# Moving four gate projections of a joint attention layer behind queries and keys on one Trainium2 core

## The reference, cut to what matters

```python
def heads_ab(pp, cq_gain, ckv_gain, w_uq, w_ukv, q_gain, k_gain, qg_gain, kg_gain):
    cq, ckv, kr, gq, gk, gv, gate = split_cols(pp, AB_SPLIT)
    qa = (rmsnorm(cq, cq_gain) @ w_uq).reshape(lead + (MLA_HEADS, MLA_NOPE + MLA_ROPE))
    kv = (rmsnorm(ckv, ckv_gain) @ w_ukv).reshape(lead + (MLA_HEADS, MLA_NOPE + MLA_V))
    ...
    return rmsnorm(qa, q_gain), rmsnorm(ka, k_gain), va, qb, kb, vb, gate

    qa, ka, va, qb, kb, vb, g = heads_ab(h @ w_in, *wts)
    qac, kac, vac, qbc, kbc, vbc, gc = heads_ab(hc @ w_in, *wts)
    ...
    oa = joint_dense_attention(qa, ka, va, kac, vac).reshape(b, s, -1)
    ob = joint_dense_attention(qb, kb, vb, kbc, vbc).reshape(b, s, -1)
    mix = jnp.concatenate([oa, ob], axis=-1) * jax.nn.silu(g)
    x = x + gate * (mix @ w_out)
```

## Time and profile before

| what | value |
|---|---|
| time, median of 3 runs | 1003.01 us (1002.25 to 1006.51) |
| span of the profiled execution | 1002.4 us |
| TensorE busy in the span | 942.2 us (94%) |
| share of the chain that ended last: PE, DVE, ACT, DMA | 84%, 5%, 4%, 4% |
| PE from 664.93 to 727.16 us (gates `ga4`, `ga5` to `ga7`) | busy throughout |
| PE from 727.16 to 736.27 us (transposes of queries and keys) | 5.06 us busy of 9.11 |
| granted clock of TensorE from 736.27 to 760 us, mean | 0.86 |

### The profile page before, as it was taken

The page is one execution under the profiler, slowest core; times in us unless marked ns, Lnnn a source line. Parts: engine busy times, 40 slices in busy tenths (PEclk is TensorE's granted clock), DMA queues, the critical chain, the costliest instruction groups (busy, mean ns, idle before and its releaser), DMA issues.

```text
span 1002.4 us, 11949 instructions
## 1 busy us (share of the span) xinstructions
PE 942.2 (94%) x4380; PEld 513.4 (51%) x4381; DVE 373.4 (37%) x838; ACT 308.4 (31%) x700; POOL 31.7 (3%) x54
## 2 busy tenths in 40 slices
PE   3899989999999899997999999999989999999998
PEld 1455446546454335442355446455766456577763
DVE  1200497634271110522122321610855633236452
ACT  3211533332131121342233321311466632125420
POOL 0100200000000000000000002000000000000000
PEclk9999999999999999999999999999989999999999
DMA  9966482489696699899799999414226734423501
GB/s 349 364 212 229 50 314 99 157 297 336 215 365 229 216 334 393 297 396 396 276 398 383 398 396 295 178 48 157 85 84 239 215 93 168 161 91 101 133 19 42
DMA packets 105693, 230.75 MB, mean 230 GB/s; under 512 B 3124, under 2 KB 6504, under 8 KB 105496
## 3 DMA queue, kind: packets, MB, share of 16 engines
q1 hardware_dynamic: 100288, 217.85, 61.5%
q0 software_dynamic: 2208, 7.37, 2.6%
q10 hardware_dynamic: 3128, 4.62, 1.4%
HBM read 224.31 MB, written 5.51 MB: 229 GB/s over the span
## 4 chain that ended last, share of the span: by engine, by line
PE 84%; DVE 5%; ACT 4%; DMA 4%; issue 2%; SPq 1%; ACTq 0%; DVEq 0%
PE bank L633 24%; PE bank L900 12%; PE bank L647 9%; PE bank L913 6%; PE bank L930 4%; PE bank L599 3%; PE bank L1208 3%; DMA arena<-in_w_mod_dram 3%; PE bank L1137 3%; PE bank L1227 2%; PE bank L1218 2%; PE bank L829 1%; PE bank L925 1%; PE bank L762 1%; PE bank L983 1%
## 5 line engine op out<-in xcount | busy, mean ns | idle before, releaser
L633 PE MATMUL bank<-arena 128*128 128x512 f32 (+3 forms) x592 | 236.6, 558 | 1.9 <-DVE arena L2687 1.0
L633 PEld LDWEIGHTS bank<-arena 128*128 128x128 f32 x592 | 111.2, 190 | 117.9 <-issue 109.1
L900 PE MATMUL bank<-arena 128*64 128x512 f32 x512 | 113.0, 593 | 3.4 <-issue 3.4
L647 PE MATMUL bank<-arena 128*128 128x256 f32 (+1 forms) x384 | 99.3, 417 | 2.8 <-ACT arena L1935 1.5
L647 PEld LDWEIGHTS bank<-arena 128*128 128x128 f32 x384 | 72.1, 190 | 30.9 <-issue 21.7
L900 PEld LDWEIGHTS bank<-arena 128*64 128x64 f32 x512 | 38.8, 137 | 73.9 <-issue 73.3
L913 PE MATMUL bank<-arena,con 128*64 128x512 f32 x272 | 65.0, 621 | 4.6 <-ACT con L1838 4.0
L599 PE MATMUL bank<-arena,silu_c 128*32 128x512 f32 x384 | 48.8, 630 | 9.5 <-DMA arena<-in_w_mod_dram 6.7
L1739 ACT ACTIVATE con<-bank 128x256 f32<-128x256 f32 x17 | 6.5, 383 | 137.3 <-PE bank L900 137.3
L2358 DVE TENSOR_TENSOR con<-con,bank 128x256 f32<-128x256 f32 x17 | 7.2, 421 | 109.5 <-ACT con L1743 109.5
L913 PEld LDWEIGHTS bank<-arena,con 128*64 128x64 f32 x272 | 21.4, 143 | 37.6 <-issue 36.5
(11 more groups left out here) (409 smaller groups left out, 1209.8 us busy)
## 6 DMA issues: line engine op xcount, KB each, us to landing
arena<-in_w_gate_e_dram SPq DMA_DIRECT2D x16, 2048.0 KB, 14.0
arena<-in_w_up_e_dram SPq DMA_DIRECT2D x16, 2048.0 KB, 13.6
arena<-in_w_down_e_dram SPq DMA_DIRECT2D x16, 2048.0 KB, 12.4
arena<-in_w_mod_dram SPq DMA_DIRECT2D x12, 2048.0 KB, 12.0
arena<-in_mod_w_dram SPq DMA_DIRECT2D x12, 2048.0 KB, 8.0
arena<-in_ab_w_in_dram SPq DMA_DIRECT2D x7, 2048.0 KB, 9.6
arena<-in_gla_w_in_dram SPq DMA_DIRECT2D x6, 2048.0 KB, 11.1
arena<-in_cd_w_in_dram SPq DMA_DIRECT2D x6, 2048.0 KB, 7.9
```

What stands on the lines that cost most here:

```text
L633: mm = pe.matmul(ps[:, 0:n], lhs[:, k, tile * P:(tile + 1) * P], w[:, k, c0:c0 + n], start=(k == 0), stop=(k == kd_ - 1))
L647: mm = pe.matmul(ps[:, i * n:(i + 1) * n], w[:, k, c * P:(c + 1) * P], rhs[:, k, 0:n], start=(k == 0), stop=(k == KC - 1))
L900: mm = pe.matmul(up_b[64 * j:64 * j + 64, :], h[:, k, :], blocks[:, g + n:u + n + 1:u - g, :], start=(k == 0), stop=(k == KC - 1), tile_po ...
```

## The change

On TensorE, `ga4` and `ga5` go from behind `c1` to behind the queries and keys of both tiles, where `ga6` and `ga7` were. `ga6` goes between the two tiles' `turn_latent`, and `ga7` behind the second. On ACT, the evictions follow that order: `ga4` is copied as before, between the latent roots of the two tiles; `gates_silu` is gone, and behind the second latent root the SiLU table is loaded, SiLU is applied in place to `ga4`'s two chunks, `ga5` is evicted with SiLU, then come `grouped_T` of both tiles, `latent_T` of tile 0, `ga6` with SiLU, `latent_T` of tile 1, `ga7` with SiLU, and the load of the logarithm-exponential table. ACT evicts the keys and values of tile 1 ahead of the latent root of tile 0. In the loads, `w_uq` and `w_ukv` go to slot 7 (held by `ab0` until `c1` has ended) in place of slot 0, at the same place of SP's queue; modulation chunk 18 now follows `ab4` in slot 0.

```diff
-        slot_turn[0] = 0
-        load("uq", a["mla_w_uq_2"][0].rearrange("(k p) c -> p k c", p=P), 2, MH * MD)
+        uq_rows = a["mla_w_uq_2"][0].rearrange("(k p) c -> p k c", p=P)
+        loads.append(("uq", [(slice(0, P), slice(0, 2), uq_rows)], 7, 2, MH * MD))
         load_ab("ab3", 1312, 512, 1)
-        w_ukv = view(slot_at(0) + 2 * MH * MD, 2, MH * P)
-        slot_turn[0] = 0
+        w_ukv = view(slot_at(7) + 2 * MH * MD, 2, MH * P)
...
-            for n in (4, 5):
-                ab_gate(n)
             for t in AB_ORDER[2:4]:
                 turned_latents(t, hT_lat)
...
             queries_keys(l0)
             queries_keys(l1)
-            ab_gate(6)
-            ab_gate(7)
+            ab_gate(4)
+            ab_gate(5)
             turn_grouped(l0)
             turn_grouped(l1)
             turn_latent(l0)
+            ab_gate(6)
             turn_latent(l1)
+            ab_gate(7)
             begin()
...
-            ab_gate(4)
-            ab_gate(5)
             for t in range(TT):
                 turned_latents(t)
...
-            def gates_silu():
-                act.wait_ge(ga_copied, 6)
-                act.preload_act_table(ACT.Silu)
-                part = gatesT[:, 4:8, 0:T]
-                act.activation(part, part, ACT.Silu).then_inc(gate4_ready, 1)
-                for n in (6, 7):
...
             queries(3)
+            keys_values(3)
             latent_head_rstd(2)
-            keys_values(3)
+            ab_gate(4, ACT.Copy)
             latent_head_rstd(3)
-            gates_silu()
+            act.wait_ge(ga_copied, 5)
+            act.preload_act_table(ACT.Silu)
+            part = gatesT[:, 4:6, 0:T]
+            act.activation(part, part, ACT.Silu).then_inc(gate4_ready, 1)
+            ab_gate(5, ACT.Silu)
             grouped_T(2)
             grouped_T(3)
             latent_T(2)
+            ab_gate(6, ACT.Silu)
             latent_T(3)
+            ab_gate(7, ACT.Silu)
+            act.preload_act_table_set(LN_EXP)
             begin()
```

More of the change, by code:

```diff
@@ L1847, in _, with ab_gate @@
                 behind_store(e)
-            def ab_gate(n):
-                c, i, half = AB_GATES[n]
+            def ab_gate(n, function):
+                c, i, _ = AB_GATES[n]
                 ps = banks.wait(act, f"ga{n}")
-                act.activation(gatesT[:, 4 * c + 2 * i:4 * c + 2 * i + 2, T * half:T * half + T],
-                               ps[:, :].rearrange("p (c t) -> p c t", c=2), ACT.Copy).then_inc(ga_copied, 1)
+                act.activation(gatesT[:, 4 * c + 2 * i:4 * c + 2 * i + 2, 0:T],
+                               ps[:, :].rearrange("p (c t) -> p c t", c=2), function).then_inc(ga_copied, 1)
             for n in (2, 3):
```

## The result

| | before | after |
|---|---|---|
| time, median (lowest to highest) | 1003.01 us (1001.58 to 1007.88) | 998.32 us (994.53 to 1003.83) |
| time of the profiled execution | not listed with its page | 998.0 us |
| span of the profiled execution | 1002.4 us | 996.2 us |
| mean granted clock of the profiled execution | 0.991 | 0.996 |

The ratio after to before is 0.995, with a 95% interval of 0.993 to 0.997: 4.7 us less, where 7.5 were forecast.

A forecast was written before the change was run, and what follows sets the result against it. TensorE bounds, with holes of 1.36 and 2.69 us before the scores and a lower clock behind them. Holes 4.05 plus clock 3.47, 7.5 us off span 1002.4, give 994.9; plus 0.6, 995.5 us; range 993.5 to 999.5.

The forecast's parts named there:

- rival 1: Ahead of and at the scores: only the two holes close, the clock term isn't gained; 999.0 us, chance 0.14.
- Part 1: Behind `c1`: the gates leave, so everything up to tile 1's keys moves forward by 13.96 us without waits.
- Part 2: Between keys and scores: gates cover the turnings, both holes close, scores start 4.0 us earlier (holes' sum 4.05).
- the slack that I put at 1.1 us: Banks of `ga5` and the first `turn_grouped`: ScalarE empties each 1.1 us before TensorE wants it; 0.65 with the dearest SiLU.
- Part 3: At the scores: without a hole the clock stays at the upper level, 5.2 us for 8.66, 3.47 saved.
- The carry: From traced span to median time: before's median lies 0.6 us above its span, added to 994.9 for 995.5.
- All later loads wait for matmuls that move along: Loads behind chunks 18 and 19: their releasing matmuls move forward too, so these loads were given no added cost.
- the signs of being wrong: Clock falling elsewhere, `ga6` or tile 0's last transposes waiting for ScalarE, or turns behind the scores waiting for VectorE.
- The clock term: At the scores: three pairs at 1.73 us each, 5.2 in place of 8.66, saving 3.47 us.
- Its first ground: Rival 1's first reason at the scores: the clock's fall isn't bound to the two holes, so 3.47 us isn't gained.
- Rival 2: From VectorE's tile 1 sums to scores: ScalarE's chain in series with gates, 19.7 us; 1008.4 if unmoved; chance 0.05.
- Rival 3: At `cT` or the queries: latents, weights or a bank hold them by the 7.5 us gained; 1003.0, chance 0.07.

The follow-up runs named there:

- the longer ones: Changed kernel with a few repeated waits on full semaphores added on TensorE, on ScalarE, or on both: 998.47, 998.89 and 996.89 us.
- the hole put back: Changed kernel with TensorE made to wait ahead of the scores for ScalarE's table load and three added copies: 1003.46 us, ratio 0.9994 to the kernel before.
- The kernel with filled holes: Kernel before with five unread matmuls put into TensorE's two holes: 1000.37 us, ratio 0.9973 to the kernel before.
- the experiment half: Changed kernel with `ga4` and `ga5` left behind `c1` and up-projection weights in slot 0: 1010.29 us, ratio 1.0072 to the kernel before.

## Why the prediction came out as it did

The mechanism held, the size didn't. The time of 998.32 us is 2.8 above the forecast's 995.5 and outside the forecast's own 993.5 to 997.5. It lies in the stated range because that was widened to rival 1, whose 999.0 it comes closer to and whose chance was put at 0.14.

**Part 1 held to a tenth.** From `cT` to `ga4` TensorE takes 34.49 us (666.57 to 701.06), and the working had 34.5 (664.9 to 699.4). `cT` waits for nothing, the up-projection weights in slot 7 are there, and VectorE's chain moved by the 14 us along with the rest. Its last latents of tile 1 are done at 718.68, 6.1 us ahead of the transposes at 724.83 (the working had 6.3). The two rows of VectorE after, the first of them to be held against the last of its kind in the earlier trace rows:

```profile
718.26 0.42 DVE L2636 TENSOR_TENSOR arena<-small,rstd 128x256 f32<-128x256 f32 x1
...
737.94 0.49 DVE L2673 TENSOR_SCALAR arena<-arena,small 128x512 f32<-128x512 f32 x1
```

**Part 2 held, slightly underrated.** From `c1`'s end to the scores it was 71.34 us (664.93 to 736.27) and is 66.92 (666.57 to 733.49): 4.42 saved, 4.05 forecast. The 0.4 is in the lengths I used. A timeline row of a merged group is longer than its share of the order, since the last matmul's end lies under the next group's start: `turn_latent` reads 1.91 and its successor starts 1.74 later, `ga6` reads 7.07 and takes 6.91. ScalarE's root of tile 1, table load, SiLU and first eviction came at 713.15, 713.91, 715.20 and 716.22, each 1.5 to 1.6 later than the working, about the 1.6 by which `c1` ended late; the slack that I put at 1.1 us was real, since `ga6` starts at 717.92 without a wait.

**Part 3 held in the trace.** 5.18 us for the scores, 5.2 forecast. VectorE's first scaling ends at 738.43 (737.94 and 0.49), 0.24 ahead of the first turned probabilities, a narrow place as the working had it (0.4). The two terms come to 4.42 + 3.48 = 7.90 where 7.5 was forecast; that is the piece's 7.99 but for 0.09 ahead of `c1`'s end.

**The step that failed is the last one, the sum itself:** that the times of the two kernels differ by these two terms alone, taken off one traced span. It fails in three places.
- *The carry.* I carried 0.6 us from span to median. In every listed execution the time lies 1.8 above its own span (998.0 and 996.2; 1008.53 and 1006.7). So before's traced execution was one of about 1004.2, 1.2 above its median, and the forecast from its span is 994.9 + 1.8 = 996.7, not 995.5.
- *Code ahead of the change.* "All later loads wait for matmuls that move along" looked behind the change only. In the changed program the code packet comes at 34 us instead of 40, its first projection starts 1.3 us later, 1.16 of it in the longer wait, and 1.7 us go to a fall of the clock there. That the clock falls at another place is one of the signs of being wrong that the prediction named; it came some 690 us ahead of the stretch that the prediction looked at. With the carry that explains the traced execution: 996.7 less 0.4 for the underrated cover, plus 1.3 and 1.7, less 1.3 for fewer falls in between (the experts' pieces, 310.80 and 312.83, and what is left of the piece before, +0.7), is the 998.0 measured.
- *The clock term over all executions.* Each listed execution has its span and its mean granted clock. Span times clock is an estimate of what the span would be without any fall: it counts half of each us at 0.50 (1.2 GHz for 2.4) as lost. Over 63 executions of before that is 993.6 us with 8.3 lost to the clock; over 38 of the changed kernel, the longer ones included, 989.75 with 6.45 lost (standard errors 0.2 to 0.4; executions of all experiments put together). So the mean spans differ by 5.7 us (standard error 0.5), well under the traces' 7.99. By the estimate 3.9 of them are won by the order, where 4.05 was forecast, and only 1.9 by the clock, where 3.47 was. The split is rough: for the hole put back, where the trace shows 4.15 us of order and 1.80 of clock, the estimate gives 2.7 and 2.9. The kernel with filled holes has 993.7, as before, and 5.75 lost, a gain of 2.6 by the clock with a standard error of 1.0, which fits 3.47 as well as 1.9.

So **rival 1 was half right**. Its first ground fell: the fall is bound to these holes (three traces of before have it, five of the changed kernel don't, filling them takes it away, one hole put back brings a shorter one back). What is left of it is that the timed executions win less than the traces show, by the estimate at the clock. Either some of them don't have that fall, or others take its place. The traces of before lost 9.0 to 14.1 us to the clock, all above the mean of 8.3, and ran longer than its median of 1002.8; so they don't stand for the median execution. All three share the falls at the scores and near 456, which cost 3.4 and 1.7 us together 5.1. Six of the 63 executions have a mean clock of 0.996, at most 4.5 us lost, so in those six at least one of the two was missing or shorter. Which one, and how it is in the other 57, stays open, since a trace exists only for these three. Its argument against itself, that the lowest run of before (1002.25) was as long as the execution with the fall, was drawn from three runs and held a time against a span; the execution with the fall is one of 1004.2, and among 63 the lowest is 999.92. The Trainium skill, "TensorE: Matmul & The Clock Gate", section "What's actually happening", has transitions shift from run to run: the falls among the experts do (at 330 in two of three traces of before), the one at the scores did not in these three.

**Rival 2** was priced at 1008.4 for a chain of VectorE that doesn't move; made so in the experiment half, it measured 1010.29 (6.3 above the median of before beside it, 5.4 forecast). The scores ran at a clock of 1.00, as it had them, but the clock fell in the holes ahead of them. In the changed kernel the rival didn't come about, because VectorE's chain moved forward by the 14 us that the gates left free ahead of `cT`. **Rival 3** is excluded by the first row of TensorE after.

By parts, from the joint pieces of one trace each: SiLU at eviction 1.70, turnings between the gates 1.60; each left out alone came back as a hole (1.54 and 1.30 us). The move of `ga4` and `ga5` is what makes both worth anything: with it left out, the same two cost 6.84.

## What to carry to other kernels

Work that nothing waits for is worth most where the engine would otherwise run dry, and moving it is safe only if the chain that it stood ahead of moves forward by the same time; price the half of the change that doesn't move that chain, it can be slower than none. A short hole ahead of dense work can have two prices, its own length and the granted clock behind it. A comparison of traces needs a table of pieces cut at rows that both programs have: here the change's own piece repeats to 0.02 us, while whole runs scatter by 9 us, and differences ahead of the change show up as such. But a trace is one execution: these three of before ran longer than the median, and the 8.0 us of the piece came to 5.7 in the mean span.

## What the runs showed of the hardware

- A hole's length alone doesn't say what it costs in clock. Two holes of 1.36 and 2.69 us with 1.92 us of transposes between them led to 0.50 in three of three traces (scores 8.64 to 8.66 us for 5.18), one of 3.99 us led to a shorter fall (6.98 us), one of 1.30 us ahead of the scores and one of 1.54 us behind them to none; the last three were seen in one trace each.
- A packet of code in the time of a weight load goes with a later landing. A 16 KB packet of 1.1 us beside 2 MB loads of weights went with a landing 1.1 us later (24.2 for 23.1), and whether it falls there changes with a few idle instructions hundreds of us later in the program. The Trainium skill, "Runtime: NRT & Kernel Launch", section "Instruction fetch mechanics", says that code comes in blocks of 16 KiB and that crossing one is mostly hidden; the packet's size agrees, and at this place it goes with a wait of 2.42 us in place of 1.26.
